# Weight sums made a stage earlier and kept in DRAM, reciprocals on a small tile, and a turn one slot later

## The chip, the cores and the metric

The kernel runs on one core of one Trainium2 chip. The metric is the device time of one execution in microseconds, as the median of several runs. TensorE (PE) does the matmuls, VectorE (DVE), ScalarE (ACT) and GpSimd (the Pool) do the rest, and SyncE (SP) issues almost all DMAs, in the order of its program. Engines run their own instruction streams in order and meet at semaphores.

## The reference, cut to what matters

Two blocks follow each other on one sequence of 2048 rows of 1024. The change touches the projection of the second block and a place in a projection of the first. The second block, cut:

```
h = rms_norm(x, norm_w) * (1 + scale) + shift
proj = h @ w_in                                  # 1024 -> 2888 columns
u_pool, g_pool, q, k, v, g_attn, qi, ki, wi = split(proj)
pool_out = pool_mixer(u_pool, w_pool, pool_scale) * silu(g_pool)
q = rope(rms_norm(q.reshape(S, 8, 64), q_norm_w)); k = rope(rms_norm(k, k_norm_w))
qi = rope(qi); ki = rope(ki)
attn_out = dsa_attention(q, k, v, qi, ki, wi) * silu(g_attn)
x = x + gate * (concat([pool_out, attn_out]) @ w_out)

def pool_mixer(u, ...):   # per group of 128 columns, window w = 2, 4, 8, 16
    pooled = (sum of the last w rows) / min(row + 1, w) - u
    return (pooled @ w_pool[group]) * pool_scale
```

## The kernel before, in words

Matmuls in full precision are done in three passes: each operand is split into a high part (ScalarE, a copy to a shorter type) and a low part (VectorE, a subtraction), and high x high, high x low and low x high are added up in PSUM.

The projection `proj` uses a two by two scheme with seven block products instead of eight. Its class is `PairSpace` (from line 1975), its programs are `rotate_programs` (line 2547). The seven products are called A11, S1, S2, A12, S3, S4, A22 after their weight factor, in the order in which TensorE does them. The factors S1 to S4 are sums of the four weight blocks a11, a12, a21, a22: S1 = a21 + a22, S2 = S1 - a11, S3 = a11 - a21, S4 = a12 - S2. A product is 12 matmuls of 128x128 on 512 columns (4 blocks of the contraction, 3 passes).

The work runs over 24 groups, 12 for each half of the rows. A group is a pair of 128 output columns (`upper` and `lower` of `Columns`); group 0 and group 12 are the narrow tails with four products. After the tail come norm, pool, norm, pool, norm, pool, norm, pool, norm, gates, gates. One pass through the loop over `g` is called a slot here: TensorE multiplies group `g`, while the other engines finish group `g - 1` (`was`) and get the weights of group `g + 1` (`nxt`) ready.

- Weights: SP loads the four blocks (`load`, lines 2051 to 2069), the Pool makes the four sums (`sum`, lines 2078 to 2096), ScalarE splits high (`split_hi`, L2107), VectorE low (`split_lo`, L2116). TensorE waits for each low part (`multiply`, L2151).
- Results: ScalarE takes `first`, `p5`, `u2` and `u3` out of PSUM (`keep_first` L2145, `keep` L2919), VectorE adds (`leave_b` L3034, `leave_c` L3039), the Pool makes the last quarter (`finish` L2801). S3 of a group waits for `u2`, A22 for `u3`.
- A norm group: ScalarE squares the upper rows (L2838) and splits the squares (L2847), VectorE makes their low part (L3043), TensorE sums them over the heads (`sum_squares` L3249, after S1 of the next slot), ScalarE takes the root (L2851), VectorE inverts a tile of 128x1024 in four pieces (`invert` L3085), turns the rows (sine L3053, cosine L3065, sum L3075) with a copy of the rows whose halves SP has exchanged by four DMAs (`swap` L2684), multiplies with the inverse (L3091), and high and low parts are stored (`take_high` L2886, `low_turned` L3097, `store_rot` L2688, `store_low` L2693).
- A pool group: VectorE sums the windows (`add_windows`), ScalarE and VectorE split them (L2857, L3139), TensorE mixes (`mix` L3260, after A12 of the next slot), ScalarE scales (`blend` L2871). Its lower rows (qi) are turned as above, without a norm (L3055, L3067, L3075).
- A gates group: two silus and two stores.

Group 13, the first whole one of the second half, needs new factors of x. They come as "late" rows from DRAM (`load_ahead`, `load_late_half`, `late_high` L2943, `late_low` L3167, the Pool's `late_difference` L2807), which slot 11 (`LAST`) begins.

Ahead of the rotation runs `out_b_programs` (line 2281), the output product of the first block: 16 row tiles, each gated (`pool_gate` L1502 on the Pool), split, multiplied (L2515), normalised twice, transposed (L2524), shifted (L2409 on ScalarE, L2475 on VectorE) and, for the first half of the rows, turned into the seven factors of x, which are split in 14 pieces (`PIECES_AT`, L2414 and L2480). The last steps already do the tail of group 0 and load the weights of group 1.

Much earlier lies `project_programs` (line 1153), another seven-product projection with 16 groups, in which the Pool has next to nothing to do.

Of the kernel before, what the change touches and what calls it, by code (L numbers as in the profile page):

```python
# [744 lines left out]
class ProjectSpace:  # L745
# [6 lines left out]
    def __init__(self, nc, sem, at_hi):  # L752
# [21 lines left out]
        self.whole = [at(f"whole{j}", offset, [P, MULTS, KH, UNIT]) for j, offset in enumerate((lo + 6 * S, rest + 11 * S))]  # L774
        small = at("small", rest + 11 * S + 7 * KB, [P, 40 + 3 * KC])
# [8 lines left out]
        self.last_out = [sem(f"pb_last_out{j}") for j in range(2)]  # L784
        self.taken, self.made, self.x1_out = sem("oa_taken"), sem("oa_made"), [sem(f"oa_x1_out{j}") for j in range(2)]

# [366 lines left out]
def project_programs(nc, sem, proj, acc, pt, weights, h_late, out_t, mod_kept, mod_row, next_space):  # L1153
# [15 lines left out]
    CHUNKS = 3 * KC  # L1169
    late_at = {divmod(MULTS * LAST + turn, MULTS): m for m, turn in enumerate((0, 2, 4, 6, 7, 8, 9))}  # L1170
# [18 lines left out]
    def sync(sp):  # L1189
# [29 lines left out]
        for g in range(GROUPS):  # L1219
# [33 lines left out]
        store_lower(END)  # L1253

    def gpsimd(pool):
        pool.wait_ge(upper_out, 16)
        for b in range(2):
            store_unit(pool, proj, h_late, PAIRS - 1, b, proj.last_out[b])

# [187 lines left out]
class SecondOutSpace:  # L1447
# [10 lines left out]
    def __init__(self, nc, sem, attention):  # L1458
# [16 lines left out]
        self.o_in, self.g_in = ([sem(f"ob_{of}_in{j}") for j in range(D)] for of in "og")  # L1475
# [11 lines left out]
    def load_outputs(self, sp, o_t, kvqg_t, n):  # L1487
        j, t = n % self.DEEP, ROWS[n]
        sp.dma_start(self.o[:, j], o_t.rearrange("(k p) (t n) -> t p k n", p=P, n=P)[t]).then_inc(self.o_in[j], 16)
        sp.dma_start(self.g[:, j], kvqg_t[3 * self.AC * P:, :].rearrange("(k p) (t n) -> t p k n", p=P, n=P)[t]).then_inc(self.g_in[j], 16)  # L1490

    def gate(self, nc, dve, n):
        j = n % self.DEEP
        dve.wait_ge(self.o_in[j], 16 * (n // self.DEEP + 1))
        dve.wait_ge(self.g_in[j], 16 * (n // self.DEEP + 1))
        nc.vector.tensor_tensor(self.o[:, j], self.o[:, j], self.g[:, j], ALU.mult).then_inc(self.gated, 1)

    def pool_gate(self, nc, pool, n):
        j = n % self.DEEP
        pool.wait_ge(self.o_in[j], 16 * (n // self.DEEP + 1))  # L1500
        pool.wait_ge(self.g_in[j], 16 * (n // self.DEEP + 1))
# [3031 lines left out]
```

## Time and profile before

| | us |
|---|---|
| median of 3 runs | 3106.57 |
| lowest, highest | 3103.05, 3109.3 |
| profiled execution, its own time | 3103.51 |
| its span in the trace | 3101.7 |

The granted TensorE clock is 0.977 of full speed as a mean over the span. Busy in the span: TensorE 2916 us, VectorE 2429, ScalarE 1747, the Pool 522. The rows below are from the profiled execution; times of day in them are microseconds from the span's start. A TensorE instruction that streams 512 columns is shown with 0.39 us, but the next one starts 0.23 us after it. Of a wait the trace names the last releaser.

### The profile page before, as it was taken

How to read it: one execution, taken by the hardware profiler on the slowest of the kernel's cores; microseconds unless marked ns; L12 is line 12 of the kernel's file. 1: busy time of each engine (PE TensorE's matmuls, PEld its weight loads, DVE VectorE, ACT ScalarE, POOL GpSimd, SP SyncE). 2: the span in 40 equal slices, each digit the busy share in tenths (PEclk: the TensorE clock that was granted, in tenths of full speed). 3: DMA queues.
4: the chain of work that ended last, by engine and by line, in shares of the span. 5: the costliest groups of instructions: out<-in, count | busy, mean ns of one | idle time of the engine just before them, and what ended most of it. 6: DMA issues, size and time to landing. Idle time of an engine off the chain costs nothing. (4 is left out here: it accounts for less than half of the span.)

```text
span 3101.7 us, 49546 instructions
## 1 busy us (share of the span) xinstructions
PE 2916.2 (94%) x17248; PEld 2326.3 (75%) x17248; DVE 2428.9 (78%) x3533; ACT 1746.5 (56%) x3207; POOL 522.3 (17%) x791
## 2 busy tenths in 40 slices
PE   6999999999999999999998898899977899999899
PEld 5888888888878886777777677677755677777687
DVE  8888887766676758889878799799768898888553
ACT  5343422232454537777767654555478899888510
POOL 2000000000000001000114333343212333243100
PEclk8999999999999999999999999999989999999999
DMA  4434422257755433111135544544471111111774
GB/s 123 124 106 128 153 68 68 68 184 258 220 153 168 144 114 102 36 37 39 46 99 192 169 150 129 171 126 155 143 146 45 25 32 28 26 39 39 166 220 140
DMA packets 414557, 355.22 MB, mean 115 GB/s; under 512 B 100738, under 2 KB 362882, under 8 KB 411876
## 3 DMA queue, kind: packets, MB, share of 16 engines
q1 hardware_dynamic: 412500, 347.79, 38.2%
q0 software_dynamic: 1088, 3.93, 0.7%
q8 instruction: 141, 2.31, 0.4%
q14 instruction: 108, 0.88, 0.1%
q10 hardware_dynamic: 720, 0.31, 0.1%
HBM read 229.13 MB, written 112.87 MB: 110 GB/s over the span
## 5 line engine op out<-in xcount | busy, mean ns | idle before, releaser
L349 ACT ACTIVATE s_mx_w_hi<-s_mx_raw 128x512 fp32r<-128x512 f32 x224 | 138.5, 628 | 310.3 <-PE p_oa_acc L705 238.0
L705 PE MATMUL p_oa_acc<-s_h_a_hi,s_mx_w_hi 128*128 128x512 f32 x744 | 291.4, 392 | 8.8 <-DVE s_h_a_lo L448 7.1
L705 PE MATMUL p_oa_acc<-s_h_a_hi,s_mx_w_lo 128*128 128x512 f32 x744 | 290.3, 390 | 0.0
L705 PE MATMUL p_oa_acc<-s_h_a_lo,s_mx_w_hi 128*128 128x512 f32 x744 | 290.2, 390 | 0.0
L2151 PE MATMUL p_pr_ps<-s_pr_x_hi,s_pr_w_hi 128*128 128x512 f32 x588 | 233.1, 396 | 13.9 <-DVE s_pr_w_lo L2116 9.0
L1825 DVE TENSOR_TENSOR_SCAN s_st_prod<-s_st_soft,s_st_prod 128x512 f32<-128x512 f32 x192 | 234.8, 1269 | 8.2 <-ACT s_st_soft L1752 7.5
L2151 PE MATMUL p_pr_ps<-s_pr_x_lo,s_pr_w_hi 128*128 128x512 f32 x588 | 231.2, 393 | 0.0
L2151 PE MATMUL p_pr_ps<-s_pr_x_hi,s_pr_w_lo 128*128 128x512 f32 x588 | 231.0, 393 | 0.0
L1752 ACT ACTIVATE s_st_soft<-p_st_z 128x512 f32<-128x512 f32 (+3 forms) x320 | 153.4, 533 | 108.5 <-PE p_st_z L1878 107.7
L4243 PE MATMUL p_sa_turn<-s_ident,s_sa_arg 128*128 128x128 f32 x1088 | 164.8, 287 | 42.3 <-ACT s_sa_prob L3841 23.0
L491 DVE TENSOR_TENSOR s_mx_w_lo<-s_mx_raw,s_mx_w_hi 128x512 fp32r<-128x512 f32 x224 | 153.3, 685 | 53.6 <-ACT s_mx_w_hi L349 52.1
L3824 ACT ACTIVATE s_sa_arg<-s_sa_arg,s_sa_low_top 128x128 f32<-128x128 f32 (+15 forms) x128 | 155.0, 1213 | 48.1 <-DVE s_sa_low_top L3976 47.8
L4243 PEld LDWEIGHTS p_sa_turn<-s_ident,s_sa_arg 128*128 128x128 f32 x1088 | 119.4, 143 | 81.0 <-issue 53.5
L705 PEld LDWEIGHTS p_oa_acc<-s_h_a_hi,s_mx_w_hi 128*128 128x128 f32 x744 | 140.2, 188 | 39.2 <-issue 10.4
L3833 ACT ACTIVATE s_sa_relu<-p_sa_pr 128x512 f32<-128x512 f32 (+3 forms) x304 | 154.5, 561 | 24.4 <-DVE s_sa_score L3957 13.4
L3957 DVE SCALAR_TENSOR_TENSOR s_sa_score<-s_sa_relu,s_sa_w_idx,s_sa_score 128x1024 f32<-128x1024 f32 (+7 forms) x154 | 153.7, 1020 | 12.6 <-ACT s_sa_relu L3833 11.4
L4257 PE MATMUL p_sa_o_sum<-s_sa_prob,s_sa_v_nat 128*64 128x128 f32 x2176 | 158.9, 286 | 4.4 <-ACT s_sa_o L3847 4.0
L705 PEld LDWEIGHTS p_oa_acc<-s_h_a_hi,s_mx_w_lo 128*128 128x128 f32 x744 | 140.1, 188 | 29.3
L705 PEld LDWEIGHTS p_oa_acc<-s_h_a_lo,s_mx_w_hi 128*128 128x128 f32 x744 | 140.3, 189 | 28.7
L4257 PEld LDWEIGHTS p_sa_o_sum<-s_sa_prob,s_sa_v_nat 128*64 128x64 f32 x2176 | 119.0, 140 | 55.4 <-issue 46.2
L3841 ACT ACTIVATE s_sa_prob<-p_sa_turn 128x512 f32<-128x512 f32 (+3 forms) x320 | 153.3, 536 | 11.0 <-PE p_sa_turn L4243 9.2
L1896 PE MATMUL p_st_turn<-s_ident,s_st_prod 128*128 128x128 f32 x1088 | 155.9, 282 | 1.8 <-DVE s_st_prod L1825 1.7
(489 smaller groups left out, 7890.3 us busy)
## 6 DMA issues: line engine op xcount, KB each, us to landing
s_mx_raw<-in_w_in_a SPq DMA_DIRECT2D x128, 256.0 KB, 3.8
s_pb_ada<-in_w_ada SPq DMA_DIRECT2D x16, 768.0 KB, 7.2
s_pr_w_a<-in_w_in SPq DMA_DIRECT2D x44, 256.0 KB, 3.2
s_pr_w_raw<-in_w_in SPq DMA_DIRECT2D x44, 256.0 KB, 3.3
d_rot_hi<-s_pr_rot SPq DMA_DIRECT2D x18, 512.0 KB, 2.7
d_y_t<-s_mx_y SPq DMA_DIRECT2D x16, 512.0 KB, 5.4
s_oa_y_raw<-d_y_t SPq DMA_DIRECT2D x16, 512.0 KB, 6.9
s_oa_x<-in_x SPq DMA_DIRECT2D x16, 512.0 KB, 4.9
```

The lines of the kernel that those rows point to most:

```text
L491: nc.vector.tensor_tensor(w_lo[:, m], raw[g % 2][:, m], w_hi[:, m].bitcast(F32), ALU.subtract).then_inc(lo_done, 1)
L705: ins = nc.tensor.matmul(bank, w[:, m, k, :], a[:, m, k, :], start=(k == 0 and n == 0), stop=(k == KH - 1 and n == 2))
L1752: nc.scalar.activation(soft[:, u % DEEP, s, 0:n], z[u % 2 * 2 + s][:, 0:n], ACT.Sigmoid, scale=-SCALE).then_inc(softened, 1)
L1825: nc.vector.tensor_tensor_scan(prod[:, b, s, 0:n][:, ::-1], back, back, carry, ALU.mult, ALU.bypass).then_inc(multiplied, 1)
L1896: ins = nc.tensor.transpose(turn[i % 2][:, c:c + P], prod[:, u % DEEP, s, c:c + P], ident[:])
L2151: ins = nc.tensor.matmul(bank, w[:, k, :], a[:, k, :], start=opens and k == 0 and n == 0, stop=k == KH - 1 and n == 2, skip_group_check=no ...
L3824: nc.scalar.activation(row, row, ACT.Exp, scale=-1.0, bias=low_top[:, s % DEEP, side, len(parts(qb)) - 1:len(parts(qb))], accum_out=total[ ...
L3833: nc.scalar.activation(relu[:, a % R_DEEP, half:half + n], pr[p % BANKS][:, 0:n], ACT.Relu).then_inc(relu_done, 1)
L3841: nc.scalar.activation(prob[:, u % P_DEEP, side, 0:w], turn[turn_of["prob", u, side] % 2][:, 0:w], ACT.Copy).then_inc(p_ready, 1)
L3957: ins = nc.vector.scalar_tensor_tensor(s, relu[:, a % R_DEEP, 0:n], w, s, ALU.mult, ALU.add)
L4243: ins = nc.tensor.transpose(turn[i % 2][:, c:c + P], arg[:, s % DEEP, side, at + c:at + c + P], ident[:])
L4257: ins = nc.tensor.matmul(o_ps[side * HD:side * HD + HD, pair * P:pair * P + P], v_nat[:, (at + c) // P, kv * HD:kv * HD + HD], prob[:, u % ...
```

## The change

1. In groups 8 to 14 of the first projection SP loads the eleven sets of four weight blocks of the second block's `w_in` (44 loads of 256 KB), the Pool makes the four sums of each, and SP stores them in DRAM (44 stores).
2. In the rotation each whole group loads seven factors (a11, a12, a22 and the four stored sums). The Pool makes no sums there; both halves of the rows read the same stored sums.
3. The root of a norm, equal for 64 rows at a time, is gathered from two rows of the wide tile onto a tile of 128x16 (two DMAs), inverted there by VectorE, stored to DRAM (one DMA) and spread back over 64 partitions each (two DMAs). The product with the inverse, and the high and low parts of the norm group, move one slot later.
4. The turn of a pool group's lower rows (sine, cosine, sum, high, low, stores) moves one slot later, and its swap goes to another tile. The mix comes after S3 instead of A12.
5. The order of the steps is changed on all engines, and weight splits of S2 and A12 are done a slot earlier.
6. In the output product the gates move from the Pool to VectorE; the pieces of x are split in another order, one for each step until step 16, six after it; SP's loads of group 1 and stores of late rows come in another order.

The core of the diff:

```
+    def sum_blocks(self, nc, pool, n):
+        a11, a21, a12, a22 = self.blocks[n % 2]
+        pool.wait_ge(self.blocks_in[n % 2], 64 * (n // 2 + 1))
+        nc.gpsimd.tensor_tensor(a22[:], a21[:], a22[:], ALU.add).then_inc(self.blocks_summed, 1)
...
+    BLOCKS_AT = {8: (0, 1), 9: (2,), 10: (3, 4), 11: (5,), 12: (6, 7), 13: (8,), 14: (9, 10)}
...
+            for n in BLOCKS_AT.get(g - 1, ()):
+                proj.store_blocks(sp, w_sums, n)
+            for n in BLOCKS_AT.get(g, ()):
+                sp.wait_ge(late_lo, AHEAD)
+                proj.load_blocks(sp, w_next, n)
...
+        if q in self.SUMS:
+            block = self.w_sums[self.whole(g) % self.w_sums.shape[0], self.SUMS.index(q)]
...
-    PIECES_AT = {9: 2, 10: 2, 11: 1, 12: 1, 13: 2, 14: 2, 15: 2, 16: 1, 17: 1}
+    PIECES_AT = {**{step: 1 for step in range(9, 17)}, 17: 2, 18: 1, 19: 2, 20: 1}
...
         store(TILES - 1)
-        pairs.load(sp, FIRST, "a12")
-        for n in range(TILES - 4, TILES):
+        sp.wait_ge(transposed, TILES - 2)
+        pairs.load(sp, FIRST, S.A22_T4)
+        for n in range(TILES - 4, TILES - 2):
             store_late(n)
+        pairs.load(sp, FIRST, S.A12_B21)
+        for n in range(TILES - 2, TILES):
+            store_late(n)
+        pairs.load(sp, FIRST, S.S3_T3)
...
```

SP's order in the slot of the rotation, after the change (`norm` and `pool` are group g - 2, if it is of that kind):

```
+            if g == LAST:
                 load_ahead()
                 load_late_half(0)
+            if was_kind in ("norm", "tail"):
                 swap(was)
+            if kinds[g] != "tail" and was_kind != "tail":
+                pairs.load(sp, g, S.A22_T4)
+            if more:
+                pairs.load(sp, nxt, S.A11_B11)
+            if norm is not None:
+                store_rot(norm)
...
+            if more:
+                pairs.load(sp, nxt, S.S1_T1)
+            if norm is not None:
+                store_low(norm)
+            if was_kind == "norm":
+                gather_roots(was)
+            if pool is not None:
+                store_rot(pool)
+            if more:
+                pairs.load(sp, nxt, S.S2_T2)
+            if pool is not None:
+                store_low(pool)
+            if was_kind == "norm":
+                store_inverse(was)
...
+            if more:
+                pairs.load(sp, nxt, S.A12_B21)
+            if was_kind == "norm":
+                spread_inverse(was)
+            if more:
+                pairs.load(sp, nxt, S.S3_T3)
+            if was_kind == "pool":
                 store_pooled(was)
+                swap(was)
...
+            if more:
+                pairs.load(sp, nxt, S.S4_B22)
```

ScalarE's order from the middle of the slot:

```
+            if norm is not None:
+                take_high(norm)
             if was_kind == "pool":
                 split_mix(was)
-                split_pooled(was)
             if whole:
                 keep_p5(g)
             if was_kind == "norm":
                 root(was)
+            if pool is not None:
+                take_high(pool)
+            if more and g:
+                pairs.split_hi(nc, act, nxt, S.A11_B11)
             if whole:
                 keep_u2(g)
+            if was_kind == "pool":
+                split_pooled(was)
...
+            if was_kind == "tail":
+                take_high(was)
             if whole:
                 keep_u3(g)
```

VectorE's order, its first half:

```
             if was_kind == "norm":
                 low_squares(was)
+            if norm is not None:
+                times_inverse(norm)
+            if was_kind == "pool":
+                add_windows(was)
             if whole:
+                pairs.split_lo(nc, dve, g, S.S4_B22)
...
             if was_kind in ("norm", "tail"):
                 times_sin(was)
+            if norm is not None:
+                low_turned(norm)
             if whole:
+                pairs.split_lo(nc, dve, g, S.A22_T4)
             if was_kind in ("norm", "tail"):
                 times_cos(was)
                 add_turned(was)
             if was_kind == "pool":
+                low_mix(was)
+            if pool is not None:
+                times_sin(pool)
+                times_cos(pool)
+                add_turned(pool)
+            if more and g:
+                pairs.split_lo(nc, dve, nxt, S.A11_B11)
+            if was_kind == "pool":
                 low_pooled(was)
+            if pool is not None:
+                low_turned(pool)
...
             if was_kind == "norm":
+                invert(was)
```

## Rows read from the trace of the kernel before

**Rows 1.** Windows by stage: stretch, length, engines' busy us, granted clock, DMA share, GB/s.

```profile
1003.00:1150.00 147.00, 147.00 (x651) 121.70 (x650) 99.35 (x142) 73.70 (x127) 0.00 (x0) 1.00 0.38 133
1590.00:1738.00 148.00, 130.07 (x662) 102.83 (x657) 114.88 (x180) 102.27 (x218) 53.61 (x39) 0.95 0.59 190
1738.00:2248.00 510.00, 468.60 (x1983) 375.61 (x1984) 441.05 (x429) 260.52 (x382) 187.06 (x107) 0.97 0.48 147
```

**Rows 2.** Waits of TensorE, 1738 to 2250: us, times, longest.

```profile
PE p_ob_pt L3260 <- issue: 15.9, 5, 5.2
PE p_pr_ps L2151 <- DVE s_pr_w_lo L2116: 9.0, 9, 3.3
PE p_ob_pt L3249 <- DVE s_pr_wide_lo L3043: 7.6, 7, 1.9
PE p_pr_ps L2161 <- issue: 5.7, 1, 5.7
PE p_pr_ps L2151 <- ACT s_pr_u L2919: 4.7, 2, 3.2
```

**Rows 3.** Lines of VectorE by form, 1736 to 2250: busy us, mean ns, idle before.

```profile
L2116 DVE TENSOR_TENSOR s_pr_w_lo<-s_pr_w_raw,s_pr_w_hi 128x512 fp32r<-128x512 f32 x110 | 97.8, 913 | 1.3 <-POOL s_pr_w_raw L2089 1.3
L3085 DVE RECIPROCAL s_pr_wide<-s_pr_wide 128x256 f32<-128x256 f32 x40 | 68.3, 1729 | 0.0
L3055 DVE TENSOR_TENSOR s_pr_wide<-s_pr_wide,s_pr_sin 128x1024 f32<-128x1024 f32 x8 | 15.2, 1900 | 0.0
```

**Rows 4.** Timeline of VectorE in slot 4: start, us, instruction, idle before.

```profile
1811.43 1.23 DVE L3043 TENSOR_TENSOR s_pr_wide_lo<-s_pr_wide,s_pr_rot 128x1024 fp32r<-128x1024 f32 x1 [2.27 <-ACT s_pr_rot L2847]
1817.85 3.36 DVE L3085 RECIPROCAL s_pr_wide<-s_pr_wide 128x256 f32<-128x256 f32 x2
```

**Rows 5.** Lines of the Pool, 1736 to 2250.

```profile
L2084 POOL TENSOR_TENSOR s_pr_w_raw<-s_pr_w_a,s_pr_w_a 128x512 f32<-128x512 f32 x21 | 40.9, 1949 | 224.8 <-DMA s_pr_w_a<-in_w_in 168.9 <-PE p_pr_ps L2151 55.9
```

**Rows 6.** DMA issues, 1736 to 2250: count, KB each, median us to landing.

```profile
s_pr_w_raw<-in_w_in SPq DMA_DIRECT2D x42, 256.0 KB, 3.3
s_pr_work<-s_pr_upper SPq DMA_DIRECT2D x40, 128.0 KB, 2.7
s_pr_x_raw<-d_rows_late SPq DMA_DIRECT2D x2, 1024.0 KB, 10.6
```

**Rows 7.** Timeline of TensorE, slot 4 and the start of slot 5.

```profile
1812.71 0.74 PE L3249 MATMUL p_ob_pt<-s_pr_rot,s_pr_ones 128*128 128x512 f32 x2 [1.10 <-DVE s_pr_wide_lo L3043]
1828.32 0.47 PE L2151 MATMUL p_pr_ps<-s_pr_x_hi,s_pr_w_hi 128*128 128x512 f32 x1 [0.78 <-DVE s_pr_w_lo L2116]
```

**Rows 8.** Timeline of ScalarE, the same slots.

```profile
1808.56 1.28 ACT L2901 ACT_TABLE_LOAD   x1
1816.69 0.60 ACT L2919 ACTIVATE s_pr_u<-p_pr_ps 128x512 f32<-128x512 f32 x1 [0.34 <-PE p_pr_ps L2151]
1827.61 1.06 ACT L2886 ACTIVATE s_pr_rot<-s_pr_upper 128x1024 fp32r<-128x1024 f32 x1 [3.83 <-DVE s_pr_upper L3091]
```

**Rows 9.** Timelines of VectorE and ScalarE, slot 1 and slot 11.

```profile
1753.10 1.22 DVE L3055 TENSOR_TENSOR s_pr_wide<-s_pr_wide,s_pr_sin 64x1024 f32<-64x1024 f32 x1 [9.66 <-DMA s_pr_wide<-s_pr_upper]
1981.01 1.92 ACT L2943 ACTIVATE s_pr_x_hi<-s_pr_x_raw 128x2048 fp32r<-128x2048 f32 x1 [5.95 <-DMA s_pr_x_raw<-d_rows_late]
1991.83 5.63 DVE L2127 TENSOR_TENSOR s_pr_w_lo<-s_pr_w_raw,s_pr_w_hi 128x288 fp32r<-128x288 f32 x2
```

**Rows 10.** Timeline of SP's queue, end of the output product.

```profile
1728.79 11.03 SPq L2331 DMA_DIRECT2D d_rows_late<-s_ob_late  x4
```

**Rows 11.** Waits of TensorE, 1590 to 1740.

```profile
PE p_ob_pt L2524 <- ACT s_ob_late L2409: 7.9, 2, 4.9
PE p_ob_pt L2524 <- ACT s_pr_x_raw L2409: 5.4, 4, 1.8
```

**Rows 12.** Lines of the Pool, 1590 to 1738.

```profile
L1502 POOL TENSOR_TENSOR s_ob_o_raw<-s_ob_o_raw,s_ob_g_raw 128x512 f32<-128x512 f32 x14 | 22.9, 1645 | 20.8 <-DMA s_ob_g_raw<-d_kvqg_t 20.7
```

**Rows 13.** Timeline of VectorE in the output product, beside the Pool.

```profile
1653.13 2.31 DVE L2453 TENSOR_TENSOR s_ob_y<-s_ob_x,s_ob_norm 128x1024 f32<-128x1024 f32 x1
```

More of the change, by code:

```diff
@@ L1253, in sync @@
         store_lower(END)
+        for j in range(2):
+            sp.wait_ge(proj.blocks_out[j], 64 * ((BLOCKS + 1 - j) // 2))
     def gpsimd(pool):
@@ L1258, in gpsimd @@
             store_unit(pool, proj, h_late, PAIRS - 1, b, proj.last_out[b])
+        for n in range(BLOCKS):
+            proj.sum_blocks(nc, pool, n)
     def scalar(act):
@@ L2027, in whole @@
         return sum(not self.is_tail(n) for n in range(g))
-    def tails(self, g):
-        return sum(self.is_tail(n) for n in range(g))
     def nth(self, g, q):
@@ L2483, in vector @@
         dve.wait_ge(norm_in, 16)
-        for i in range(STEPS):
+        for i in range(STEPS + 1):
             if 0 <= i - 1 < TILES:
@@ L2738, in sync @@
             was, nxt = g - 1, g + 1
+            was_kind = kinds[was] if g else "none"
+            more = g > 0 and nxt < N and kinds[nxt] != "tail"
+            norm, pool = older(g, "norm"), older(g, "pool")
             if g == LAST:
@@ L2741, in sync @@
                 load_late_half(0)
-            if g and kinds[was] != "gates":
+            if was_kind in ("norm", "tail"):
                 swap(was)
-            if nxt < N and nxt > 1 and kinds[nxt] != "tail":
-                for which in ("a21", "a22", "a11"):
-                    pairs.load(sp, nxt, which)
-            if g and kinds[was] == "tail":
+            if kinds[g] != "tail" and was_kind != "tail":
+                pairs.load(sp, g, S.A22_T4)
+            if more:
+                pairs.load(sp, nxt, S.A11_B11)
@@ L2754, in sync @@
+            if norm is not None:
[10 more added lines that the diff above has]
+                store_inverse(was)
             if g == LAST:
                 load_late_half(1)
-            if nxt < N and nxt > 1:
-                if kinds[nxt] == "tail":
-                    for h in range(2):
-                        pairs.load_tail(sp, nxt, h)
-                else:
-                    pairs.load(sp, nxt, "a12")
@@ L2762, in sync @@
-            if g and kinds[was] == "pool":
+                for h in range(2):
+                    pairs.load_tail(sp, nxt, h)
+            if more:
+                pairs.load(sp, nxt, S.A12_B21)
+            if was_kind == "norm":
+                spread_inverse(was)
+            if more:
+                pairs.load(sp, nxt, S.S3_T3)
+            if was_kind == "pool":
                 store_pooled(was)
-            if g and kinds[was] != "gates":
+                swap(was)
+            if was_kind == "tail":
@@ L2815, in gpsimd @@
         pool.wait_ge(ones_ready, 4)
-        for n in range(1, 3):
-            pairs.sum(nc, pool, 1, n)
-        pool.wait_ge(out.transposed, TILES)
-        pairs.sum(nc, pool, 1, 3)
         for g in range(1, N):
-            nxt = g + 1
-            more = nxt < N and kinds[nxt] != "tail"
-            if more:
-                for n in range(3):
-                    pairs.sum(nc, pool, nxt, n)
             if kinds[g] != "tail":
@@ L2829, in gpsimd @@
                 late_difference()
-            if more:
-                pairs.sum(nc, pool, nxt, 3)
     def scalar(act):
         def square(g):
-            posted(act, g)
+            act.wait_ge(roots_in, 32 * norms_to(g))
+            act.wait_ge(turned, before("tail", g))
             act.wait_ge(b_left, g + 1)
@@ L2950, in scalar @@
             was_kind = kinds[was] if g else "none"
+            norm, pool = older(g, "norm"), older(g, "pool")
             more = nxt < N and kinds[nxt] != "tail"
@@ L3172, in vector @@
             was_kind = kinds[was] if g else "none"
+            norm, pool = older(g, "norm"), older(g, "pool")
             more = nxt < N and kinds[nxt] != "tail"
```

307 lines of the change are left out of this document (144 added, 163 removed).

## The prediction

> **What bounds the kernel now.** I read the windows by stage first, since only time in which TensorE stands still, or runs at its lower clock, can be won. In the stage of the first projection that the change touches (1003 to 1150 us) TensorE never stops; in the second output product (1590 to 1738) it is busy 130 of 148 us, and in the seven-product projection (1738 to 2248) 469 of 510 at a granted clock of 0.97 [rows 1]. TensorE's waits in the last of these add up to 44.7 us: 15.9 before the pooling's mix, 9.0 for low halves of weights, 7.6 for the low half of the squares, 5.7 before the tail product, 6.3 for kept sums, 0.2 without a cause [rows 2] (the 0.2 and 1.6 of the 6.3 are smaller rows of that view). All but the last few have VectorE behind them: it is busy 441 of the 510 us [rows 1]. That load is inflated. Forty reciprocals of 128x256 take 68.3 us, and two-operand passes are drawn out while the Pool works: the low halves of summed weights take 913 ns on average and the sine products 1900 ns [rows 3], where a pass of 128x1024 beside an idle Pool takes 1.23 us [rows 4]. The Pool makes four weight sums per group, of up to 1.95 us [rows 5]. So VectorE and the Pool set this stage's loss, and its ceiling is the 44.7 us plus what the lower clock costs: 0.97 over 510 us is 30 us at half speed, most of which falls on the stops themselves; I estimate 8 us of lost work.
>
> **The change part by part.** *Sums out of the rotation.* 84 Pool passes (21 of the first of four) [rows 5] go, and with them ScalarE's and VectorE's waits on them. In their place come three more loads of 256 KB per group (seven instead of four). A load lands 3.3 us after its issue [rows 6], in most cases more than half a slot before TensorE wants the block; I cost them at nothing as long as SP's queue reaches them in time.
>
> *Reciprocals.* The 68.3 us on VectorE become ten passes of 128x16. The trace has none of that shape; each lies between nothing and the 1.7 us of 128x256 [rows 3], and I take 0.2, since it has a sixteenth of the columns. VectorE's load in this stage falls by 66 us, and by some 45 us of stretching, from 441 to about 330 of 510. Each norm then needs five small DMAs in three hops. The swap's DMAs, the nearest row, land after 2.7 us [rows 6], so three hops are about 8 us; the product with the inverse is put a slot later, so this fits.
>
> *The order of a slot.* The rest is a question of who is late next, and I follow one pair of slots. Five products and four sum matmuls take 15.6 - 0.8 = 14.8 us [rows 7], so a product takes 2.78 and a slot 19.5, with 0.93 for the squares' sums or 1.4 for a mix. ScalarE sees a product 0.27 us after its last matmul's turn: 1812.71 + 0.93 + 2.78 = 1816.42, and it starts at 1816.69 [rows 7, 8].
> In the slot after a pooling group (its group is a norm) I find no stop: the windows' sums come first on VectorE, need 3.0 to 7.2 us, the pooled low half is ready at about 12 to 14 us, and the mix, now after S3, comes at 14.
> In the slot after a norm (pooling groups, and the first gates group) I find a new one. Its clock: S4 of the norm ends at -2.78, the upper half is complete at -2.78 + 0.27 + 0.65 = -1.85, the square takes 1.06, and from the table load to the low squares it is 2.87 us [rows 4, 8], so the low squares start at 2.2. From there to the end of the turned sum the trace needs 6.42 us (1811.43 to 1817.85, where the reciprocals begin) [rows 4]; then come the older pooling group's sine, cosine and sum, 3 x 1.15 = 3.5, which end at 12.1. ScalarE's high half of that group (1.06) [rows 8] ends at 13.1, and behind it in ScalarE's order stand one weight split and the copy of U2, which ends near 14.2. TensorE wants S3, which waits for that copy, at 4 x 2.78 + 0.93 = 12.05. That is a stop of 2.1 us in eight slots, 17 us. Its bounds are 0 (VectorE catches up by 2 us) and 3.5 (the three passes are stretched).
>
> *The rest of the stage.* In slot 1 the tail's high half now stands ahead of U3. The tail's swap landed at 1753.1 [rows 9], 15 us into the slot, behind 2 MB of tables, and I expect the same, so U3 is there at 21 instead of 16.8: 4.2 us in place of 1.7. In slot 11 the load of A22 is now behind 3.25 MB of late rows; a part of them landed 10.6 us after its issue [rows 6], and ScalarE waited until 1981.01 for it [rows 9]. ScalarE's order makes U2 wait for that block too: 2.4 us in place of 3.2. The tail's low halves took 5.63 us beside a Pool pass [rows 9]; the Pool's own sum there remains, but VectorE is earlier: 3 in place of 5.7. Slot 13's 1.6 goes. The start: TensorE waited 3.3 us for the first low half, because SP held the stores of late rows behind a load that waits for the tail's second product (four stores, 11 us) [rows 10]. Two of the four now go first: 3.3 us won. The waits for A11's low half (0.8 each) [rows 7], the squares and the mix go. What stays is 17 + 4.2 + 2.4 + 3 = 26.6 of 44.7: **18 us won**, and 2 more from the clock, as the stops over 3 us become fewer.
>
> *Output product.* Its TensorE waits are 5.4 + 7.9 us [rows 11], with some 4 us of lower clock behind them. Fourteen gates leave the Pool, 1.65 us each [rows 12], and cost VectorE some 0.65 each (half of the 1.23 of 128x1024, and a little for stretching) [rows 4], 9 us. Five of the splits of x move from the steps of the products to those after them, 5 x 1.23 = 6 us back on VectorE; a pass that met the Pool took 2.31 instead of 1.23 [rows 4, 13]. VectorE about breaks even, ScalarE gains 5 us. I take **8 us won** of 17; the bounds are -3 (VectorE takes the gates fully) and 13.
>
> *First projection.* Forty-four Pool passes and 22 MB of DMA come in. From 1003 to 1150 VectorE is busy 99 of 147 us and the DMA engines 38% [rows 1]. Stretching of 0.4 to 1.1 us per Pool pass (441 us of the rotation hold about 45 for 107 passes; 2.31 - 1.23 is the most) makes 18 to 47 us, against 48 us of idle VectorE; the DMA share, at 133 GB/s now, goes to some 0.8 with 150 more. I take **1.5 us lost**, between 0 and 30. The Trainium skill, on its page "SBUF — State Buffer" (section "SBUF: two separate sides"), says that VectorE passes with two SBUF inputs and the Pool take an exclusive lock on a shared port pair, and that the loser stands fully still. By that rule the price per Pool pass would be its whole length, and the rotation would win more as well. The rows show doubling, not a full stop of every pass, so I stay with them.
>
> Sum: 18 + 2 + 8 - 1.5 = 26.5 us. The profiled execution took 3103.51 us, its span 3101.7; the three timed runs have their median at 3106.57, so the profile is the quicker end of normal. 3103.5 - 26.5 = 3077.
>
> **Rivals.** *No stop at U2.* VectorE reaches the older pooling group earlier than I have it, and the 17 us go as well; then 3077 - 17 = 3060, and 3055 with the output product at its better end. For it: VectorE stands idle before the low squares, so a small change of timing pays. Against it: the order is fixed and each step has its row.
> *SP's queue becomes the bound.* Behind the norm's hops SP takes loads in order: the block of S3 waits for the inverse's store to land and the broadcast to go out. If a hop takes 5 us instead of 2.7, the next slot's VectorE chain starts 2.5 us late and the mix stops by as much, eight times: 3077 + 20 = 3097. For it: in-order waits held those four stores for 11 us [rows 10]. Against: half a slot is spare.
> *The first projection stops (slower).* Place: VectorE there. If each of the 44 Pool passes holds it for the 1.95 us that a Pool pass lasts, 86 us meet 48 idle, and 38 us come onto TensorE: 3077 + 38 = 3115. It decides as soon as a pass costs VectorE over 1.1 us. By the lock rule of the Trainium skill's page "SBUF — State Buffer", taken to its end, it comes out so; no row of this kernel shows a cost so high.
> *The change doesn't do what it says*: TensorE's stops merely change owner and the time stays at 3100 to 3106.
>
> **How the numbers follow.** Forecast 0.45, no stop at U2 0.20, SP's queue 0.15, owner change 0.08, first projection 0.12. About 0.2% (6 us) is what a measurement of this kernel can tell from no change. Faster by more holds the first three: 0.80; same 0.08; slower 0.12. The range runs from 3055, the second case's better end, to 3099, the third case and the forecast with the output product at its worse end.
>
> **What would show it.** VectorE busy some 330 us in the rotation and no stretched weight splits; no TensorE waits for the mix, the squares or A11; eight waits of about 2 us for U2 with ScalarE's high half just before it; the first low half in time; TensorE still unbroken from 1003 to 1150. I am wrong if U2 is in time, if SP's loads come after ScalarE asks for them, or if TensorE stops in the first projection.

## The result, and the profile after

The changed kernel takes 3116.75 us (median of 8 runs, 3113.05 to 3122.52) where the kernel before takes 3106.27: a ratio of 1.0038, with a 95% interval of 1.0028 to 1.0048. It is **slower by 0.4%**; 3077 us were forecast. The profiled execution took 3122.52 us (span 3120.7), the slow end of its runs, and that of before the quick end of its own, so the stages below differ by 19.0 us in sum and the medians by 10.5. In the profiles of four experiments that leave the rotation's slots as changed (but for the end of the last in one of them) the rotation takes 521.5 to 531.2 us (529.8 here), so of the sum several us are spread between runs. The kernel before has one profile.

The span cut at TensorE's first instruction of each stage:

| stage | before | after | difference | forecast |
|---|---|---|---|---|
| up to the attention's first turn | 1168.26 | 1171.94 | +3.7 | +1.5 |
| first attention | 431.35 | 431.45 | +0.1 | 0 |
| second output product | 138.43 | 125.57 | -12.9 | -11.3 |
| rotation | 510.54 | 529.79 | +19.3 | -16.7 |
| wait before the selecting attention | 5.87 | 12.60 | +6.7 | 0 |
| rest | 847.25 | 849.35 | +2.1 | 0 |

(The stop of 3.3 us at the rotation's start lies ahead of its first product and so counts with the output product here.) The windows of the changed kernel that answer to [rows 1], and then the output product and the rotation of the kernel before, cut at the same places; the columns are the same:

```profile
1003.00:1150.00 147.00, 147.00 (x650) 121.78 (x649) 118.36 (x141) 73.70 (x127) 61.42 (x41) 1.00 0.88 277
1603.39:1728.96 125.57, 117.39 (x560) 93.27 (x561) 110.47 (x184) 95.41 (x205) 26.25 (x20) 0.99 0.72 230
1728.96:2258.75 529.79, 481.54 (x1985) 387.10 (x1983) 334.21 (x403) 264.55 (x385) 40.29 (x23) 0.94 0.60 180
```

```profile
1599.61:1738.04 138.43, 121.81 (x561) 96.21 (x561) 110.05 (x174) 97.47 (x209) 53.45 (x38) 0.95 0.63 203
1738.04:2248.58 510.54, 469.18 (x1984) 375.75 (x1984) 441.01 (x429) 260.48 (x381) 187.06 (x107) 0.97 0.48 147
```

VectorE fell from 441 to 334 us in the rotation, as forecast (330), and the first projection is unbroken. But TensorE stands still for 529.79 - 481.54 = 48.3 us of the rotation (before 510.54 - 469.18 = 41.4), and the same matmuls take 12.4 us longer (481.54 less 469.18), at a granted clock of 0.94 instead of 0.97. Its waits there, to be read against [rows 2]:

```profile
PE p_pr_ps L2143 <- ACT s_pr_u L2969: 38.0, 12, 5.0
PE p_sa_turn L4232 <- PEq L4508: 12.6, 1, 12.6
PE p_pr_ps L2153 <- issue: 4.8, 1, 4.8
PE p_pr_ps L2143 <- ACT s_pr_first L2137: 2.7, 1, 2.7
PE p_ob_pt L3310 <- issue: 1.5, 1, 1.5
PE p_pr_ps L2153 <- ACT s_pr_first L2137: 1.2, 1, 1.2
```

The many waits for VectorE are gone, and twelve for copies of U2 and U3 stand in their place. Eight of these are the slots that were forecast, the ones after a norm. One of them, on VectorE, ScalarE and TensorE:

```profile
1799.42 1.23 DVE L3098 TENSOR_TENSOR s_pr_wide_lo<-s_pr_wide,s_pr_rot 128x1024 fp32r<-128x1024 f32 x1 [3.47 <-ACT s_pr_rot L2895]
1801.76 1.28 DVE L3108 SCALAR_TENSOR_TENSOR s_pr_work<-s_pr_work,s_pr_norms_s,s_pr_sin 128x1024 f32<-128x1024 f32 x1 [0.52 <-DMA s_pr_work<-s_pr_upper]
1803.97 0.69 DVE L2108 TENSOR_TENSOR s_pr_w_lo<-s_pr_w_raw,s_pr_w_hi 128x512 fp32r<-128x512 f32 x1 [0.93 <-ACT s_pr_w_hi L2103]
...
1809.42 1.23 DVE L3130 TENSOR_TENSOR s_pr_lower<-s_pr_lower,s_pr_work 128x1024 f32<-128x1024 f32 x1
```

```profile
1803.31 0.63 ACT L2103 ACTIVATE s_pr_w_hi<-s_pr_w_raw 128x512 fp32r<-128x512 f32 x1 [2.40 <-DMA s_pr_w_raw<-in_w_in]
...
1810.68 1.06 ACT L2936 ACTIVATE s_pr_rot<-s_pr_lower 128x1024 fp32r<-128x1024 f32 x1 [3.83 <-DVE s_pr_lower L3130]
1811.65 0.61 ACT L2103 ACTIVATE s_pr_w_hi<-s_pr_w_raw 128x512 fp32r<-128x512 f32 x1
1812.17 0.58 ACT L2969 ACTIVATE s_pr_u<-p_pr_ps 128x512 f32<-128x512 f32 x1
```

```profile
1812.80 0.70 PE L2143 MATMUL p_pr_ps<-s_pr_x_hi,s_pr_w_hi 128*128 128x512 f32 x1 [3.62 <-ACT s_pr_u L2969]
1813.29 0.63 PE L2143 MATMUL p_pr_ps<-s_pr_x_lo,s_pr_w_hi 128*128 128x512 f32 x1
```

ScalarE's order is plain: it idles 3.83 us for the older pooling group's turned sum (1809.42 + 1.23), makes its high half, splits a weight, and only then copies U2, for which TensorE has waited 3.62 us. Two idle times stand in VectorE's chain ahead of that: 0.52 for the swap and 0.93 for a weight's high half, whose block reached ScalarE 2.40 us late. The eight slots side by side (us; VectorE's idle times are those between the low squares and the pooled sum):

| U2 at | stop | VectorE idle for swap and weight | stop less that |
|---|---|---|---|
| 1812.80 | 3.62 | 1.45 | 2.17 |
| 1858.62 | 3.49 | 1.19 | 2.30 |
| 1904.77 | 2.81 | 0.62 | 2.19 |
| 1952.84 | 3.98 | 2.09 | 1.89 |
| 2090.19 | 3.85 | 1.66 | 2.19 |
| 2136.64 | 2.88 | 0.70 | 2.18 |
| 2182.17 | 3.20 | 0.93 | 2.27 |
| 2229.81 | 4.01 | 2.21 | 1.80 |
| sum | 27.84 | 10.85 | 16.99 |

What is left in the last column, 2.1 per slot and 17 in sum, is the forecast to the tenth; the 10.85 come on top, and all of them are waits for what SP's queue brings: 4.5 us for the swap and 6.3 for high halves of weights whose blocks were late. At the end of the rotation that queue is late as well:

```profile
2247.97 1.42 SPq L2719 DMA_DIRECT2D d_rot_lo<-s_pr_upper  x1
2254.77 0.62 SPq L2832 DMA_DIRECT2D s_sa_wi_raw<-d_p_t  x2
```

The selecting attention's twenty-four first loads, 0.6 us each to issue, begin at 2254.77, once the last norm's low half has landed, because that norm's product with the inverse now comes a slot later. In the kernel before they began at 2237.35:

```profile
2237.35 0.62 SPq L2776 DMA_DIRECT2D s_sa_wi_raw<-d_p_t  x2
```

The same at the end of the first projection, where the stores of the last eight sums wait for the Pool and the first attention's loads stand behind them; the last row is the first of these loads in the kernel before:

```profile
1149.64 7.14 SPq L818 DMA_DIRECT2D d_w_sums<-s_pb_block  x8
1156.87 0.50 SPq L1587 DMA_DIRECT2D s_st_k_raw<-d_kvqg_t  x1
```

```profile
1149.76 0.32 SPq L1550 DMA_DIRECT2D s_st_k_raw<-d_kvqg_t  x1
```

### The profile page after: what moved, and what is told of

Its sections match the earlier page's. It is cut to its first block and busy times, and to the rows that moved or that the text cites. A ratio compares the mean times of both kernels' runs of the same rounds, so it can differ in the third digit from the quotient of the medians.

```text
span 3120.7 us, 49553 instructions
## 1 busy us (share of the span) xinstructions
PE 2931.9 (94%) x17248; PEld 2343.2 (75%) x17248; DVE 2340.8 (75%) x3517; ACT 1748.7 (56%) x3207; POOL 411.8 (13%) x733
## 5 line engine op out<-in xcount | busy, mean ns | idle before, releaser
L2143 PE MATMUL p_pr_ps<-s_pr_x_hi,s_pr_w_hi 128*128 128x512 f32 x588 | 240.8, 409 | 40.7 <-ACT s_pr_u L2969 38.0
L2143 PE MATMUL p_pr_ps<-s_pr_x_lo,s_pr_w_hi 128*128 128x512 f32 x588 | 238.3, 405 | 0.0
L2143 PE MATMUL p_pr_ps<-s_pr_x_hi,s_pr_w_lo 128*128 128x512 f32 x588 | 237.9, 405 | 0.0
L2108 DVE TENSOR_TENSOR s_pr_w_lo<-s_pr_w_raw,s_pr_w_hi 128x512 fp32r<-128x512 f32 x154 | 107.6, 702 | 112.5 <-ACT s_pr_w_hi L2103 112.4
L2143 PEld LDWEIGHTS p_pr_ps<-s_pr_x_hi,s_pr_w_hi 128*128 128x128 f32 x588 | 116.2, 198 | 71.2 <-ACT s_pr_u L2969 43.0
L2103 ACT ACTIVATE s_pr_w_hi<-s_pr_w_raw 128x512 fp32r<-128x512 f32 x154 | 95.2, 625 | 126.1 <-DMA s_pr_w_raw<-d_w_sums 88.9
```

Source lines behind the costliest of these rows:

```text
L2143: ins = nc.tensor.matmul(bank, w[:, k, :], a[:, k, :], start=opens and k == 0 and n == 0, stop=k == KH - 1 and n == 2, skip_group_check=no ...
```

## The experiments

**The theory** from these rows: ScalarE's order at U2 makes the eight stops, late loads lengthen them, and each long stop also costs clock. Its rival: SP's in-order queue is the limit, and U2 only the place where it shows.

**U2 first.** In `scalar`:

```diff
-            if pool is not None:
-                take_high(pool)
             if more and g:
                 pairs.split_hi(nc, act, nxt, S.A11_B11)
             if whole:
                 keep_u2(g)
+            if pool is not None:
+                take_high(pool)
```

> The changed kernel with one step of ScalarE's order moved: the high half of the older pooling group stands behind the copy of U2 instead of ahead of it and of the split of A11. Theory (order): that high half makes the eight stops of 2.8 to 4.0 us (27.8 us in the profile), each with a stretch at the lower clock behind it. All eight go, about 28 us of stops and 8 to 10 us of clock, and the time falls from 3117 to 3072 to 3085. Rival (SP's queue): weights and swaps come too late by themselves, and VectorE with them; then TensorE stops in the same slots for a low half of A11 or S1 instead, and the time stays at 3100 to 3115.

Measured: 3116.93 us, no change from the changed kernel's 3116.75 (ratio to before 1.0034, 1.0021 to 1.0047). The waits of TensorE in the rotation:

```profile
PE p_pr_ps L2143 <- ACT s_pr_u L2969: 29.1, 12, 8.6
...
PE p_pr_ps L2143 <- ACT s_pr_first L2137: 8.0, 6, 3.1
PE p_ob_pt L3310 <- issue: 8.0, 4, 3.5
PE p_pr_ps L2153 <- issue: 5.1, 1, 5.1
```

In those eight slots U2 itself is in time now; the stops moved 5 us on, to U3, and to the copy of A11's product and the mix. The sum of all is 51.3 us, where it was 48.3. ScalarE and SP's queue in the slot shown above:

```profile
1816.81 0.63 ACT L2103 ACTIVATE s_pr_w_hi<-s_pr_w_raw 128x512 fp32r<-128x512 f32 x1 [3.43 <-DMA s_pr_w_raw<-d_w_sums]
1817.35 0.58 ACT L2969 ACTIVATE s_pr_u<-p_pr_ps 128x512 f32<-128x512 f32 x1
```

```profile
1812.89 0.33 SPq L2714 DMA_DIRECT2D d_rot_hi<-s_pr_rot  x1
1813.26 0.43 SPq L2091 DMA_DIRECT2D s_pr_w_raw<-d_w_sums  x1
```

A weight load stands behind the store of the pooling group's high half and so waits for VectorE's whole chain; ScalarE waits for the load, and U3 for ScalarE. The theory in its first form fell.

**Loads ahead of stores, with and without U2 first.** In `sync`, the loads of S2, A12 and S3 ahead of what waits for this slot's results:

```diff
-            if pool is not None:
-                store_rot(pool)
             if more:
                 pairs.load(sp, nxt, S.S2_T2)
-            if pool is not None:
-                store_low(pool)
-            if was_kind == "norm":
-                store_inverse(was)
...
                 pairs.load(sp, nxt, S.A12_B21)
-            if was_kind == "norm":
-                spread_inverse(was)
+            if pool is not None:
+                store_rot(pool)
             if more:
                 pairs.load(sp, nxt, S.S3_T3)
+            if pool is not None:
+                store_low(pool)
+            if was_kind == "norm":
+                store_inverse(was)
...
+            if was_kind == "norm":
+                spread_inverse(was)
```

> The kernel with U2 copied ahead of the older pooling group's high half, and in addition another order of SP's queue in a slot: the weight loads of S2, A12 and S3 stand ahead of the stores of that pooling group and of the store and broadcast of the norm's inverse. With U2 first alone, the stops moved from U2 to U3, to the copy of A11's product and to the mix, because ScalarE waited 2 to 4 us for weight blocks. Theory now (two limits in a row): SP's in-order queue is the second, since a load behind a store waits for what the store waits for, ScalarE's high half of the pooling group and the hops of the inverse. Then most of the stops outside slots 1, 11 and 12 go: the rotation falls from 525 to 500 to 508 us, and the time from 3117 to 3090 to 3100. Rival: the loads are late by their own landing time (the DMA engines move 180 GB/s here instead of 147), and the order changes nothing: 3112 to 3120.

> The changed kernel with only the new order of SP's queue (loads ahead of the pooling group's stores and of the inverse's store and broadcast), U2 still behind the high half. Theory: ScalarE's order still makes its part of the eight stops, about 2.1 us each; what lies above that (0.6 to 2.2 us) comes from late loads and goes in part: 27.8 us of stops fall to 17 to 22, time 3108 to 3113. Rival: the stops hang on SP's queue alone; then they go here as well, and the time is that of the kernel with both edits.

Measured: both edits 3100.71 us (0.998 of before, 0.997 to 0.999), the rotation 507.95 us; the new order alone 3127.55 (1.0076, 1.0055 to 1.0098). The waits with both edits, then with the order alone:

```profile
PE p_ob_pt L3310 <- issue: 17.3, 6, 3.9
PE p_pr_ps L2143 <- ACT s_pr_u L2969: 12.1, 4, 6.2
```

```profile
PE p_pr_ps L2143 <- ACT s_pr_u L2969: 36.6, 12, 6.0
PE p_ob_pt L3310 <- issue: 12.0, 5, 3.7
```

With both, the eight stops and those that had replaced them at U3 are gone (in slot 11 the one at U2 grew from 2.2 to 6.2 us), and time and rotation lie at the edge of what was expected: two limits stood in a row, and neither edit gains alone. For the order alone I had expected 17 to 22 us at U2 and a gain; the eight stops fell only to 23.2 (2.0 to 3.5 each), and five stops before the mix came in. That was a miss: the blocks of A22 and S4 and the swap, on which VectorE waits in those slots, are not among what was moved. In both kernels the order sends the inverse out last, and VectorE waits 4.1 to 7.1 us for it in each of ten slots, ahead of the sums that the mix needs. One of these with both edits:

```profile
1823.36 1.23 DVE L3141 TENSOR_TENSOR s_pr_upper<-s_pr_upper,s_pr_inverse 128x1024 f32<-128x1024 f32 x1 [6.61 <-DMA s_pr_inverse<-d_inverse_row]
```

**The inverse's product after the windows' sums.** The row above names the next owner: the product waits 6.61 us at the head of VectorE's slot, and the windows' sums, which need nothing of it, queue behind. On top of the four edits (both above and the two of the hand-overs below), in `vector`:

```diff
-            if norm is not None:
-                times_inverse(norm)
             if was_kind == "pool":
                 add_windows(was)
+            if norm is not None:
+                times_inverse(norm)
```

> All four edits: U2 first, loads ahead in SP's queue, the last sums' stores behind the attention's first loads, and the attention's first loads of the next stage ahead of the last stores. Theory: the parts add: the two hand-overs give 2.6 and 8 us in their stages, the rotation 20 to 25: 3080 to 3092, faster than the kernel before (3105.7) by 0.4 to 0.8%. Rival: what is won early in the rotation is waited for again at its end; then above 3100.

> The kernel with all four edits, and in addition VectorE's product with the inverse behind the sums over the windows in the slot after a pooling group. With loads ahead in SP's queue the stops at U2 and U3 were gone and six before the mix were left (15.8 to 17.3 us), with VectorE idle 6.6 us ahead of that product for the broadcast of the inverse. Theory: the product was ahead of work that could be done in that time; the mix stops go, 13 to 16 us with 2 to 4 of clock, 3094 to 3075 to 3080. Rival: the high and low half of the norm's rows then come later, and with them the pooled low half, which the mix waits for as well; then the mix stops stay over 10 us in sum, and the time is 3088 to 3096.

Measured: the four edits 3093.93 us (0.9958, 0.9945 to 0.9971); with this one 3076.67 (0.9898, 0.9882 to 0.9915). The four edits lie just above their range (3080 to 3092), and the fifth inside its own: the waits for the mix fell from 15.8 to 2.8 us, and the rotation takes 491.3 us:

```profile
1727.70:2219.02 491.32, 462.68 (x1985) 373.71 (x1983) 339.29 (x403) 263.06 (x385) 40.76 (x23) 0.98 0.66 196
```

This is the time that was forecast for the change, reached with three changes of order in SP's queue, one on ScalarE and one on VectorE. That the numbers agree is luck in part: the 17 us at U2 that the forecast kept are gone here, and slot 11 with the tail behind it stops for 17.8 us (7.7, 5.0 and 5.1) where the forecast had 5.4.

**The two hand-overs.** The stores of the last sums behind the attention's first loads; and eight of the selecting attention's loads ahead of the last norm's stores, with waits only for what they read and overwrite:

```diff
-            for n in BLOCKS_AT.get(g - 1, ()):
+            for n in BLOCKS_AT.get(g - 1, ()) if g < END else ():
                 proj.store_blocks(sp, w_sums, n)
...
         next_space.load_first(sp, out_t, (upper_out, 16 * END), product, MULTS * END)
+        for n in BLOCKS_AT[END - 1]:
+            proj.store_blocks(sp, w_sums, n)
```

```diff
...
+            if g == N - 1:
+                first_loads()
+                load_some(8)
             if norm is not None:
                 store_rot(norm)
+                if g == N - 1:
+                    store_low(norm)
...
```

> The changed kernel with the last eight stores of weight sums in the first projection moved behind the attention's first eight loads in SP's queue. Theory: the stores, which wait for the Pool until 1155 us, hold those loads from 1150 to 1157, and the attention starts 3.8 us late because of that (TensorE's waits at its start 4.1 and 2.6 us instead of 3.2 and 0.9); these return to the values of before, 3.5 to 4 us less, 3113. Rival: the 22 MB of DMA traffic themselves make the loads slow; then the waits stay above 5.5 us in sum, and the time changes by less than 1.5 us.

> The changed kernel with SP's order at the end of the rotation changed: eight of the attention's twenty-four first loads go out before the last keys' turned rows are stored, these rows' high and low half are stored next to each other, and the rest of the loads wait only for what they read and overwrite. Theory: the hand-over to the attention (TensorE idle for 12.6 us, 5.9 in the kernel before) is set by SP's queue, which issues 24 loads of 0.6 us each only once the last low half has landed; it falls to 4 to 6 us, and the time by 7 to 9, to 3108 to 3110. Rival: the last group's own sums and stores set it, because VectorE's sum waits for the same buffer; then it falls by at most 3 us.

Measured: 3115.72 (1.0029, 1.002 to 1.0038) and 3112.54 (1.0023, 1.0012 to 1.0034). The waits of the first attention's start, before and then with the stores behind; and that of the selecting attention's start with the loads early:

```profile
PE p_st_z L1878 <- PEq L4457: 3.2, 1, 3.2
...
PE p_st_turn L1904 <- DVE s_st_v_step L1807: 0.9, 1, 0.9
```

```profile
PE p_st_z L1917 <- PEq L4510: 3.9, 1, 3.9
...
PE p_st_turn L1943 <- DVE s_st_v_step L1846: 0.2, 1, 0.2
```

```profile
PE p_sa_turn L4256 <- PEq L4532: 4.6, 1, 4.6
```

SP's order is shown as the cause at both places: 4.1 us in sum is the value of before (3.2 + 0.9) again, and 4.6 is below its 5.9. Of the second the profiles vary: the eight kernels here without this edit have 9.9 to 12.9 us there, the four with it 4.6 to 7.6. The forty-four Pool sums and 22 MB of traffic then cost TensorE nothing: it reaches the attention's first turn at 1167.89 us, before at 1168.26. The whole time fell by 1.0 and 4.2 us, less than the waits of these profiles (2.6 and 8.0), and less than expected (3.5 to 4, and 7 to 9); single runs of one kernel lie 9 to 10 us apart, so what the edits are worth in the whole time is not shown any closer.

**Slot 11.** The block of A22 ahead of the late rows, alone; and, on top of all edits so far, together with U3 copied ahead of the late rows' high halves:

```diff
             if g == LAST:
+                pairs.load(sp, g, S.A22_T4)
                 load_ahead()
...
             if g == LAST:
+                keep_u3(g)
                 late_high(0)
                 late_high(1)
```

> The changed kernel with one load moved in slot 11: the block of A22 goes out ahead of the late rows. Theory: the late block holds ScalarE 5.7 us, with it the high and low half of the keys' turned rows, with these their store, and the store holds VectorE's first sum of the slot by 6.1 us, because it writes into the buffer that is being stored; so the stops of 2.2 and 5.0 us in slot 11 go, and part of the 4.8 before the tail product: 9 to 13 us with the clock, 3104 to 3108. Rival: the late rows, now one load later, are what the end of the slot waits for; the stop before the tail grows by what is won ahead of it, and the time stays within 3 us of 3117.

> The kernel before this one with two steps in slot 11: the load of A22 ahead of the late rows, and U3 copied ahead of the late rows' high halves. Theory: slot 11 loses 6.2 us at U2 to that load and 3.8 to 9.0 at U3 to ScalarE's order; both go, and the stop before the tail product (5.7) grows by some of it, since its rows come no earlier: 4 to 9 us less than without the two steps. Rival: the late rows (3.25 MB, 7 to 10 us of landing each) set the end of slot 11 in any order; then the stop before the tail takes up all of it and the time is the same within 3 us.

Measured: alone 3117.15, no change (the rival's time, but another road: the stop before the tail grew only from 4.8 to 5.7); with both steps on top 3068.85 (0.9873, 0.9857 to 0.9889), **the fastest kernel of the study**, 1.3% below the kernel before. Alone, the stop of 2.2 us at U2 went and the one at U3 grew from 5.0 to 9.0, because VectorE stood like this:

```profile
1978.99 0.69 DVE L3090 TENSOR_TENSOR s_pr_upper<-p_pr_ps,s_pr_first 128x512 f32<-128x512 f32 x1 [11.71 <-DMA d_rot_lo<-s_pr_upper]
```

The store of the norm's low half, issued at 1966.78, went out beside 3.25 MB of late rows and mix weights, and the next group's sum is written into the buffer being stored. With U3 ahead in ScalarE's order TensorE runs on, and the wait collects before the tail product (12.7 us, one stop in place of three); what is gained is 7.8 us, inside the forecast of 4 to 9. Whether the late rows could be split up so that the 12.7 goes too was not tried.

**The output product.** The gates back on the Pool; and the splits of x as they were spread before:

```diff
+            if EARLY <= i + 2 < TILES:
+                n = i + 2
+                pool.wait_ge(space.o_g_in[n % D], 32 * (n // D + 1))
+                nc.gpsimd.tensor_tensor(space.o[:, n % D], space.o[:, n % D], space.g[:, n % D], ALU.mult).then_inc(space.gated, 1)
...
-            if EARLY <= i + 2 < TILES:
-                space.gate(nc, dve, i + 2)
```

```diff
-    PIECES_AT = {**{step: 1 for step in range(9, 17)}, 17: 2, 18: 1, 19: 2, 20: 1}
+    PIECES_AT = {9: 2, 10: 2, 11: 1, 12: 1, 13: 2, 14: 2, 15: 2, 16: 1, 17: 1}
```

> The changed kernel with the fourteen gates of the second output product back on the Pool (PIECES_AT, SP's order and everything else as changed). Theory: the gates on the Pool hold VectorE's passes and ScalarE's operands, and their move is most of what this stage won: it goes from 125.6 us to 131 to 135, the time rises by 5 to 10. Rival: the respreading of the splits and SP's order won it; then the stage stays within 2 us of 125.6.

> The changed kernel with PIECES_AT of the second output product as in the kernel before (gates on VectorE as changed). With the gates back on the Pool the stage kept its 125.5 us, so their move is not what won there. Theory: the respread splits of x are: five splits in the steps with products hold ScalarE's shifted copies; the stage goes from 125.6 to 131 us or more. Rival: the first product's weight sum that left the Pool, and SP's order of the late stores at the end, won it; then the stage stays within 2 us of 125.6 until the first product of the rotation.

Measured: 3117.8 us and 3127.53 (1.0062, 1.0045 to 1.0079). The stage's windows:

```profile
1602.82:1728.27 125.45, 116.00 (x561) 91.85 (x562) 104.35 (x170) 93.95 (x205) 46.21 (x34) 1.00 0.72 230
```

```profile
1603.05:1736.59 133.54, 119.61 (x561) 94.91 (x561) 114.36 (x190) 99.61 (x213) 25.81 (x20) 0.96 0.69 217
```

Which engine makes the gates doesn't matter here (my theory for them fell); the spread of the splits is worth 8.0 of the 12.9 us. The other 4.9 holds the stop of 3.3 at the rotation's start; what the rest is was not tried.

## Why the prediction was wrong

*What bounds the kernel, and where the load goes.* Right. VectorE's 441 us fell to 334, the low halves of weights take 702 ns instead of 913 [rows 3], and the waits for mix, squares and weight halves went from 29.2 (15.9 + 7.6 + 9.0 less the 3.3 of the start) [rows 2] to 1.5 us.

*The eight stops.* Place, order and number were right, and the 2.1 us too. The step that failed is "most cases more than half a slot before TensorE wants the block; I cost them at nothing as long as SP's queue reaches them in time": the queue did not. The block of A22 can go out only when its buffer is free, at the slot's start, and there it stands behind four swap DMAs of 0.6 us each; ScalarE waited 1.5 to 2.5 us for it in each of the eight. SP's queue in the slot shown above, the swap and then A22 with the next A11:

```profile
1796.80 2.41 SPq L2689 DMA_DIRECT2D s_pr_work<-s_pr_upper  x4
1799.24 1.23 SPq L2091 DMA_DIRECT2D s_pr_w_raw<-in_w_in  x2
```

Of VectorE's 10.85 us, 3.25 are for A22's halves, 3.07 (in four of the slots) for those of S4, whose load goes out last in the slot before, and 4.53 for the swap itself. That made 3.5 of 2.1. A swap also lands 3.3 us after its issue, before 2.7 [rows 6]; how much of the 4.53 is the queue's order and how much the landing is not shown. I had SP's queue as a rival, at 2.5 us a slot on top of the 3077, but by another road, slow hops of the inverse and a stop before the mix; the hops came as forecast in sum (below), and what came late cost 1.4 us a slot, at U2.

*The clock.* Booked as 2 us won, it lost 12.4 in this pair of profiles. Two steps failed. "As the stops over 3 us become fewer" did not come true: they are eight now, and five before (behind the start). And of the lower clock the prediction wrote "most of which falls on the stops themselves"; most of it falls behind them, on work. The windows before, in and after the stop of 3.62 us:

```profile
1796.00:1809.10 13.10, 13.10 (x58) 10.54 (x57) 8.21 (x8) 8.40 (x11) 0.00 (x0) 1.00 0.63 186
1809.18:1812.80 3.62, 0.01 (x1) 0.01 (x1) 1.95 (x3) 2.12 (x4) 0.00 (x0) 1.00 0.07 26
1812.80:1816.30 3.50, 3.50 (x9) 2.76 (x10) 2.72 (x6) 1.09 (x2) 0.00 (x0) 0.52 0.95 329
```

A granted clock of 0.52, which is TensorE's lower level, 1.2 GHz, for nearly all of the 3.5 us, is 1.7 us of work lost behind one stop. The Trainium skill ("TensorE: Matmul & The Clock Gate", section "HAM oscillation — how this bites in real kernels") describes that pattern, waits between bursts of matmuls and each burst starting slow again; the trace agrees for the long stops. Over the 6 us behind a stop the granted clock is 0.50 to 0.75 after all thirteen stops of 2.2 to 5.0 us, and 1.00 after the three of 0.8 to 1.5. In the kernel before it is 0.65 to 0.73 after the five stops of 3.1 to 5.7 us behind the start, and 1.00 after the others, all of 1.9 us or less. So how the waits were cut counted, and not only their sum. But the 12.4 is the far end of its spread: in other profiles of the same slots stops of 2.8 us (loads early) and 3.0 us (gates on the Pool) were followed by a clock of 1.00, and in the four experiments named at the start the same matmuls took 473.3 to 479.3 us, 4 to 10 more than before. The rotation with the gates on the Pool, and that of the fastest kernel, where few stops are left:

```profile
1728.27:2251.96 523.69, 476.57 (x1985) 383.19 (x1983) 333.92 (x403) 263.68 (x385) 40.78 (x23) 0.95 0.61 183
```

```profile
1726.53:2209.91 483.38, 460.26 (x1985) 373.09 (x1983) 333.75 (x403) 264.14 (x385) 36.98 (x23) 0.98 0.67 200
```

*Slots 1, 11 and 12.* Forecast 4.2 + 2.4 + 3 = 9.6 us; measured 2.7 + 2.2 in slot 1, 2.2 + 5.0 in slot 11, 4.8 at the tail and 1.2 in slot 13 (forecast to go): 18.1. Slot 1 came near its 4.2 by luck: U3, where the stop was forecast, is in time; the stops are 2.7 for the copy of A11's product and 2.2 at U2, where ScalarE waits 7.4 us for the block of A22. Missing in slot 11 were the 5.0 at U3 and its cause, the buffer. "The product with the inverse is put a slot later, so this fits" followed the data to its use and not the buffer to its next writer: group g's upper rows are stored in the slot in which group g + 2 writes there. Where SP's queue is late (slot 11, and the last slot) VectorE waits for that store, 6.1 and 6.5 us.

*The end of the rotation.* Not costed at all, 6.7 us: the last step that was moved a slot later ended in the queue of the next stage's loads. Of a step that is moved, its last instance should have been followed to the end of the program.

*First projection.* No loss inside, as forecast. VectorE's time rose from 99.35 to 118.36 us beside 41 Pool passes [rows 1], 0.46 us for each; a Pool pass took 61.42 / 41 = 1.5. The slower rival wanted over 1.1 and is out, and so is, for this stage, the reading of the Trainium skill's page "SBUF — State Buffer" (section "SBUF: two separate sides") by which every Pool pass costs VectorE its whole length; whether the two lock each other out pass by pass is not settled by a mean. The 3.7 us are SP's queue at the seam.

*Output product.* -12.9 against -11.3, by the splits and not by the gates.

*The hops of the inverse* land after 1.9, 2.3 and 4.0 us, 8.2 in sum, where "about 8" was forecast; the sum is right, its parts are not (2.7 was taken for each):

```profile
s_pr_roots<-s_pr_wide SPq DMA_DIRECT2D x20, 4.0 KB, 1.9
d_inverse_row<-s_pr_roots SPq DMA_DIRECT2D x10, 8.0 KB, 2.3
s_pr_inverse<-d_inverse_row SPq DMA_DIRECT2D x20, 256.0 KB, 4.0
```

The sum: -26.5 + 21.6 (stops in the rotation, 48.2 for 26.6) + 14.4 (clock, -2 to +12.4) + 6.7 + 2.2 - 1.6 + 2.2 (rest, unexplained, and rounding) = +19.0, the difference of the spans. By the medians it is 10.5, and the spread of the clock between profiles is about the size of the gap.

## What to carry to other kernels

When a bound engine is relieved, look at the in-order queues next: every load behind a store inherits the store's wait, and moving one of two queues that hold each other gains nothing until the other moves too (here 0 and +11 us alone, -16 together). A step moved a slot later holds its buffer a slot longer and ends a slot later: follow its last instance into the next stage, and its buffer to the next writer. And count how a wait is cut, not only its sum: 47 to 52 us of stops in sixteen to eighteen pieces cost 4 to 12 us more of clock, over five profiles, than 41 us in twenty-five pieces.

## What the runs showed of the hardware

A DMA of 4 KB takes 1.9 us to land and one of 8 KB to DRAM 2.3, hardly less than the 128 KB swap (2.7 before, 3.3 here): small transfers are paid by their number. The Trainium skill ("DMA: Bandwidth & Descriptors", section "Anatomy of one DMA — SWDGE (gpsimd) path") gives about 2.0 us of fixed cost for each, for another issuing path; the trace agrees in size. And a store of 512 KB, which lands after 3.1 us at the median here, took 12 beside 3.25 MB of loads. And the length of a stop of TensorE alone did not settle the clock behind it: a stop of 2.81 us was followed by 0.72 over 6 us in the changed kernel's profile, one of 2.82 us in the same slots by 1.00 with the loads early.
